# A two-layer decoder step on one core: seven block products for the second input projection, two of four weight sums on GpSimd

## What is computed

```python
def ret_project(h, w_in, pos):
    proj = h @ w_in                       # (tokens, 2048) @ (2048, 12288)
    q = rotate(proj[..., :2048].reshape(b, s, 8, 256), pos)
    k = rotate(proj[..., 2048:4096].reshape(b, s, 8, 256), pos) * 256 ** -0.5
    v = proj[..., 4096:8192].reshape(b, s, 8, 512)
    g = proj[..., 8192:]

def retention_chunk(s_prev, q, k, v, log_g):      # prompt: 4 chunks of 128; sample: one of 8 tokens
    scores = einsum('bhid,bhjd->bhij', q, k) * decay
    o = scores @ v + (q @ s_prev) * exp(log_g * (i + 1))
    s_new = exp(log_g * c) * s_prev + (k * exp(log_g * (c - 1 - i))).T @ v

def ret_output(o, g, w_out):
    return (head_rms_norm(o) * silu(g)) @ w_out   # (tokens, 4096) @ (4096, 2048)
```

## Time and profile before

| | |
|---|---|
| median of 3 runs | 3610.52 us (3608.27 to 3620.78) |
| span of the profiled execution | 3613.4 us |
| PE busy | 3486.5 us (96%), 26244 matmuls |
| DVE busy | 1666.8 us (46%) |
| ACT busy | 980.5 us (27%) |
| POOL busy | 68.1 us (2%) |
| DMA | 642.60 MB, 178 GB/s on average |
| chain that ended last | PE 87%, DVE 4%, DMA 3% |

### The profile page before, as it was taken

How to read it: one execution, slowest core, us unless ns; L and a number is a source line. 1 busy time by engine, 2 the same in 40 slices (tenths; PEclk the granted TensorE clock), 3 DMA queues, 4 the chain that set the end, 5 groups by cost and what they waited for, 6 DMA issues and landing times.

```text
span 3613.4 us, 65176 instructions
## 1 busy us (share of the span) xinstructions
PE 3486.5 (96%) x26244; PEld 3103.5 (86%) x26244; DVE 1666.8 (46%) x2689; ACT 980.5 (27%) x1552; POOL 68.1 (2%) x87
## 2 busy tenths in 40 slices
PE   7999999999999999888999999999999999999998
PEld 7987887788788877588999898989899999989998
DVE  4466566655666665355233333333232423333345
ACT  4222223222222232124222222222222222332123
POOL 1000000000000000002000000000000000000000
PEclk9999999999999999999999999999999999999999
DMA  5466888888888888744425252524243434433333
GB/s 175 154 203 214 269 281 258 261 286 265 262 266 282 279 256 278 223 144 142 132 83 168 82 170 82 172 85 164 88 156 93 153 99 144 157 128 105 108 123 123
DMA packets 472175, 642.60 MB, mean 178 GB/s; under 512 B 35649, under 2 KB 294850, under 8 KB 468738
## 3 DMA queue, kind: packets, MB, share of 16 engines
q1 hardware_dynamic: 407122, 565.91, 48.8%
q10 hardware_dynamic: 64336, 72.24, 6.0%
q0 software_dynamic: 416, 0.28, 0.1%
HBM read 566.09 MB, written 70.65 MB: 176 GB/s over the span
## 4 chain that ended last, share of the span: by engine, by line
PE 87%; DVE 4%; DMA 3%; issue 2%; ACT 2%; SPq 1%; ACTq 0%; POOL 0%; DVEq 0%; POOLq 0%
PE low_banks L1004 68%; PE high_banks L1004 16%; PE high_banks L1007 3%; DMA area<-in_cache_v 2%; DVE WL L1565 1%; SPq L949 1%; DVE area L1661 1%; ACT WH L1285 1%; DMA WR<-in_w_in_attn 0%; ACT area L1348 0%; DVE area L1634 0%; ACT XH L1285 0%; DVE area L1946 0%; DMA area<-in_cache_k 0%; DVE XL L1570 0%
## 5 line engine op out<-in xcount | busy, mean ns | idle before, releaser
L1004 PE MATMUL low_banks<-XH,WH 128*128 128x288 f32 (+2 forms) x6656 | 1524.8, 307 | 43.7 <-DVE XL L1570 18.4
L1004 PE MATMUL low_banks<-XH,WL 128*128 128x288 f32 (+2 forms) x6656 | 1457.1, 297 | 0.0
L1004 PE MATMUL low_banks<-XL,WH 128*128 128x288 f32 (+2 forms) x6656 | 1455.2, 296 | 0.0
L1004 PEld LDWEIGHTS low_banks<-XH,WH 128*128 128x128 f32 x6656 | 1082.7, 190 | 194.2 <-issue 148.9
L1004 PEld LDWEIGHTS low_banks<-XL,WH 128*128 128x128 f32 x6656 | 1087.1, 190 | 0.0
L1004 PEld LDWEIGHTS low_banks<-XH,WL 128*128 128x128 f32 x6656 | 1085.7, 190 | 0.0
L1565 DVE TENSOR_TENSOR WL<-WR,WH 128x1024 fp32r<-128x1024 f32 x436 | 528.7, 1213 | 753.8 <-ACT WH L1285 749.2
L1285 ACT ACTIVATE WH<-WR 128x1024 fp32r<-128x1024 f32 x436 | 461.4, 1058 | 1144.4 <-PE low_banks L1004 897.9
L1004 PE MATMUL high_banks<-area 128*32 128x256 f32 (+9 forms) x4720 | 630.4, 466 | 35.1 <-DMA area<-in_cache_v 16.8
L1004 PEld LDWEIGHTS high_banks<-area 128*32 128x32 f32 (+3 forms) x4720 | 271.6, 138 | 249.6 <-issue 177.5
L1661 DVE STREAM_TRANSPOSE area<-area 128x512 f32<-128x512 f32 x512 | 335.5, 691 | 121.2 <-PE high_banks L1004 63.2
(11 more groups left out here) (122 smaller groups left out, 928.6 us busy)
## 6 DMA issues: line engine op xcount, KB each, us to landing
area<-in_cache_k SPq DMA_DIRECT2D x512, 256.0 KB, 5.0
area<-in_cache_v SPq DMA_DIRECT2D x512, 256.0 KB, 5.5
WR<-in_w_in_ret SPq DMA_DIRECT2D x200, 512.0 KB, 3.6
WR<-in_w_in_attn SPq DMA_DIRECT2D x136, 512.0 KB, 5.5
out<-area ACTq DMA_DIRECT2D x73, 512.0 KB, 3.0
WR<-in_w_out_ret SPq DMA_DIRECT2D x68, 512.0 KB, 3.5
area<-in_state_ret SPq DMA_DIRECT2D x64, 512.0 KB, 5.5
WR<-in_w_out_attn SPq DMA_DIRECT2D x32, 512.0 KB, 5.4
```

The source lines that it names most:

```text
L1004: return nc.tensor.matmul(out, a, b, start=start, stop=stop, skip_group_check=True)
```

## The change

The input projection's 42 middle steps (all but the first three and the last three) are each done as **seven products of blocks** in place of eight. Weights of a step: 2048 rows by 256 columns as four blocks of 1024 x 128 (a11, a12, a21, a22); tokens: blocks by 1024 rows and 288 tokens. Four sums of weight blocks (s1 = a21 + a22, s2 = s1 - a11, s3 = a11 - a21, s4 = a12 - s2) and four sums of activation blocks (t1 to t4, made once) feed seven products of 8 x 3 = 24 matmuls; drains add up the four output blocks. DVE makes s2 and s4, POOL makes s1 and s3. The 48 outputs go to DRAM (`mixed_d`) and every head's q, k, v and g are loaded back. So all retention work moves behind the products: its table is 64 tiles per head now, and it lies beside the last three steps and the output projection, which has 8 parts of 512 rows (one per head), 7 of them added by DVE.

```diff
+PRODUCTS = ("a11", "s2", "s1", "s3", "a12", "s4", "a22")
+X_OF = (0, "t2", "t1", "t3", 1, 2, "t4")
+BANK_OF = (0, 1, 2, 1, 0, 2, 1)
+FILL = 96
+PER_HEAD = 64
...
+    def split(self, m):
+        n, i = divmod(m, 7)
...
+        if i == 0:
+            out += self.sum(n, "s2")
+        if i == 4:
+            out += self.sum(n, "s4")
+        if i == 5:
+            out += self.sum(n + 1, "s1")
+        if i == 6:
+            out += self.sum(n + 1, "s3") + self.load()
...
+def layer_one_inputs(prods, after):
+    out = []
+    for m in range(prods.count):
+        out += prods.split(m + 2) + prods.product(m) + after.get(prods.count - m, [])
...
+    for which in range(2):
+        for part in range(3):
+            put(-12 + early + 5 * which + 2 * part, Stage("rope", which=which, part=part))
...
-    put(129, Stage("rs_keys"))
-    put(138, Stage("pad_rows"))
-    put(152, Stage("rs_mask"))
+    put(12, Stage("rs_keys"))
+    put(13, Stage("pad_rows"))
+    put(21, Stage("rs_mask"))
     for c in range(4):
-        put(139 + 12 * c, Stage("ret_scores", c=c))
-        put(144 + 12 * c, Stage("ret_out", c=c))
-        put(146 + 12 * c, Stage("ret_state", c=c))
...
+        put(14 + 9 * c, Stage("ret_scores", c=c))
+        put(17 + 9 * c, Stage("ret_out", c=c))
+        put(18 + 9 * c, Stage("ret_state", c=c))
...
     for t in range(4):
-        put(195 + 2 * t, Stage("ret_norm", t=t))
-        put(200 + 6 * t, Stage("gate", t=t))
...
+        put(50 + t, Stage("ret_norm", t=t))
+        put(52 + 3 * t, Stage("gate", t=t))
...
     for g in range(2):
         for e in range(2):
-            put(254 + 6 * (2 * g + e), Stage("rs_state", g_=g, e=e))
+            put(56 + 3 * (2 * g + e), Stage("rs_state", g_=g, e=e))
         for j in range(4):
-            put(262 + 16 * g + 4 * j, Stage("store_state", b=2 * j + g))
+            put(61 + 7 * g + 2 * j, Stage("store_state", b=2 * j + g))
+    if h < HEADS:
+        kt = CH * (h % 2)
+        put(72, Stage("load_x", part=h % 2, kt=kt, row=CH * h, width=T, layer=1))
+        for k in range(CH):
+            put(78 + 2 * k, Stage("split_x", part=h % 2, kt=kt + k, width=T))
...
+          24: lambda: n.scale(4), 25: lambda: rec((0, 0), 2, "pool"), 26: lambda: rec((1, 0), 4, "pool"),
+          36: lambda: n.transpose(4), 40: lambda: rec((1, 1), 3, "dve"), 46: lambda: rec((0, 1), 1, "dve"), 52: lambda: mix(3),
+          54: lambda: prods.load() + prods.load(), 58: lambda: mix(1),
+          64: lambda: mix(2), 70: lambda: mix(4)}
...
+            def product(g, i, bank_, slot, ready, freed, mixed, opening):
+                pe.wait_ge(sem["w_lo"], c.after(ready, "w_lo"))
...
+                (wh, wl), (xh, xl) = ring(slot), tokens(X_OF[i])
+                for k in range(8):
+                    for n, (a, x) in enumerate(((wh, xh), (wh, xl), (wl, xh))):
+                        last = mm(bank[bank_][:, 0:HALF], a[:, k, :], x[:, k, :], start=i < 3 and k == 0 and n == 0, stop=k == 7 and n == 2)
+                last.then_inc(sem["w_used"], 1)
...
+                dve.wait_ge(sem["pool_sums"], c.before("pool_sums"))
+                v.tensor_tensor(a11, first_sum if what == "s2" else a12, a11, SUB).then_inc(sem["quad_sums"], 1)
...
+                if what == "s1":
+                    nc.gpsimd.tensor_tensor(first_sum, a21, a22, ADD).then_inc(sem["pool_sums"], 1)
+                else:
+                    nc.gpsimd.tensor_tensor(a21, a11, a21, SUB).then_inc(sem["pool_sums"], 1)
```

More of the change, by code:

```diff
@@ L232, in tile @@
             out.append(Stage("evacuate", cb=cb, pieces=a["pieces"], **kinds))
+            if cb and a["pieces"][-1][2] == T and kinds.get("row") is not None:
+                self.stores[kinds["row"]] = out[-1]
             for b, _, _ in a["pieces"]:
@@ L748, in hybrid_step_kernel @@
         AREA = 31900
+        mixes = under("mixes", [128, 8, 8, HALF], f32r)
         area = sb("area", [128, AREA])
```

524 lines of the change are left out of this document (393 added, 131 removed).

## The result

The changed kernel takes 3741.8 us (median of 4 runs, 3733.8 to 3744.7) beside 3609.4 us for the kernel before (3606.9 to 3620.8): a ratio of 1.036, 95% interval 1.034 to 1.038. It is slower by 132 us where 3617 us and "the same" were forecast, and outside the range of 3555 to 3690.

What follows compares the result with a forecast made beforehand. PE alone was taken to bound the input projection, by its count of matmuls. The terms -134 + 91 + 22 + 13 + 6 - 14 + 14 + 8 gave +6 us: 3617 against the median, range 3555 to 3690.

Steps and rivals of the forecast that it cites:

- Part 1: Input projection's products: 42 steps lose 24 matmuls each at 0.133 us, PE covering all other engines' work; -134 us.
- Rival D: Products lose pace because POOL sums hold DVE splits; 1 us a step, 42 us, giving 3660; chance 0.08.
- Part 2: End of a head's retention, tiles 50 to 66: PE waits for DVE's chain, 13 us for six heads; +91 us.
- Part 3: Head's start, tiles 13 to 17: `ret_out` waits behind padding copies, gated-row copy, `kd` and split; 2.7 us each, +22 us.
- Part 4: Activation block sums beside the first split steps: DVE and queue 8 us, POOL 5; +13 us, bounds 5 and 25.
- Part 5: Seam between products and retention: waits for last stores, state loads ahead of a weight chunk; +6 us, 0 to 12.
- Part 6: Output projection: the 14 us of stalls for splits of loaded rows go away; -14 us.
- Part 8: DMA from a head's tile 61 to 88: 13.6 MB in about 38 us, 358 GB/s against 339 seen; +8 us.
- rival C: A head's gated rows come late, ACT standing at `split_x`; 8 us for 7 heads, 3673; chance 0.22.
- Part 7: Clock falls after PE's stalls at the heads' ends: one fall of 0.17 of 10 us per head; +14 us, 0 to 30.

Runs made afterwards that it cites:

- split_late: Changed kernel with only the four splits of a head's gated rows moved from its tiles 78 to 84 to tiles 87 to 93; 3651.5 us (1.011).
- the best kernel: Changed kernel with rotation 13 tiles later, gated-row splits 9 tiles later, first weight-quad loads six tiles apart, four norms together at tile 48; 3592.4 us (0.995).

## Why the prediction was wrong

*Part 1 was right*: 0.132 us a matmul, which makes 133 us of 134, a step 22.2 us, nothing of DVE, ACT or POOL showing. Rival D fell with it.

*Part 2* had the place and the total: 91 us forecast, 88.3 found (81.7 of PE waiting for norms, updates and gates, 6.6 for ACT). The agreement is partly luck. The sum took all of DVE's work there as one chain that PE waits out. By it, moving 8.5 us of rotation out of seven heads had to give nearly all of 59.5 us of waits; it gave 23.2, less 7.0 for the rotation. And the norms moved forward gave 14 us while DVE's work stayed the same. So much of the wait comes from what stands in front of what, and not from the sum of durations; and it was named after the norms first (45.6 us), not after updates and gates as I had written.

*Part 3* had the right sequence and the wrong bound. In the changed kernel PE has no wait for `kd` at all, because the copies run in parallel with the landing of the rows, and only the later of the two is paid. With the splits out of the way it shows: 6.1 us for 22.

*Part 4* was low: 25.9 us for 13, just beyond the 25 that I had named. The hold by GpSimd is full and real (12.10 us for two splits), but taking it away gained nothing that can be measured; the 4 MB in the weight queue, which I had let fall in with DVE's lateness, gave 9 us when spread. The clock, which wasn't in this part, took another 9.

*Part 5* was about right, 6.9 for 6. *Part 6* named the right waits: those for splits were 12.7 us before (3210 us to the end) and 3.5 are left in the whole output projection. But other small ones came in their place, so the 14 us were not gained.

*Part 8 is the step that failed*, 68 of the 113 us by which the sum was too low. It set 13.6 MB against 38 us, found that the mean rate (358 GB/s) was a little above the most that I had seen (339), and charged 8 us in all for the difference. The mean was never the bound: over the 40 us from 3020 to 3060 it is 248 GB/s, with 125 and 187 in the first two stretches and 330 and 352 in the last two. What is urgent is issued in the dense half. The first state load, g, the rows and the next state loads are issued within 6 us of each other, beside the stores, and the rows share the engines with all of it for 14.8 us. An average over 38 us says nothing on when one particular megabyte lands. And the sum had no term for the place at which ACT, DVE and PE begin to wait for it: 9.5 us in each head, 76.2 in place of 8. The store of the last gated tile, on which I built rival C's 20 us road, lands 2.0 us after its issue (DMA view, 2950 to 3100 us), 8 us before the rows are asked for; the road is the read alone. Rival C had the place right (SP's queue, tile 72, ACT at `split_x` with `kd` behind; not the weights, since PE's next chunk was ready, and without the counter), its price of 8 us was near the 9.5 measured (in eight heads, not seven), and by its point of decision (more than 3 us after the copies are issued; here 4.7) it had to come. It had a chance of 0.22. At its own price the time would have been 3673, within the range.

*Part 7 failed beside it and made the time leave the range.* One fall per head at 0.17 of ten microseconds was 14 us; it is 51 in the output projection. I had read the price from a short stall and not asked what a long one does: with a stall of 9 us the clock goes to 0.59 for the ten microseconds after. And it grows with the stalls: in `split_late` 73.4 us less of waiting took 17.5 us of busy time along. The Trainium skill's rule on the shared ports, which I weighed in part 4, was right in kind, and irrelevant to the time.

## What to carry to other kernels

When a change packs work that was spread out, look for the transfer that is issued last in the burst and is needed first, add up all the bytes in flight in the microseconds between, and place the first instruction that waits for it behind that sum; an in-order engine that waits early costs all its queue. Look too at what a shared counter makes an engine wait for: here PE's wait at a new weight chunk counted row splits that it did not need for another 16 tiles. Here nine tiles of distance gave back 90 us, and rearranging three more places in tables turned 3742 us into 3592, without touching the work itself. Where waits run side by side, only removing the last one pays. And a wait of TensorE costs more than itself, in the clock that follows: from the changed kernel to the best one its idle time falls by 104 us (318.5 to 214.4) and its busy time, for the same instructions, by 42 (3413.5 to 3371.4).

## What the runs showed of the hardware that I had not expected

- A DVE instruction with two operands in SBUF that starts under a running GpSimd one doesn't slow down, it waits for the rest of it: 2.44 us for a split of 1.23, ending 1.07 us after the sum. One with an operand in PSUM isn't held (0.46 us in both cases).
- Issuing a DMA is not free when the engines are full: 2.6 to 3.9 us on SP for one that otherwise takes 0.37 us, and everything behind it in SP's program is late by as much.
- The same load of 1.15 MB takes 8.6, 12.8 or 14.8 us from issue to landing by what else is in flight (3.75 MB of stores less; 4 MB of loads later; both there).
- The granted clock was 0.59 in the ten microseconds after a stall of 9 us, 0.91 on average over the output projection, and 0.98 there in the best kernel, where the long waits are gone and the short ones left.
